# Two transformer blocks on one core: a new order of steps, the residual on VectorE, and GpSimd's low parts in halves

## The chip, the cores and the metric

The kernel runs on one NeuronCore of a Trainium2 chip, in one launch. Its engines are TensorE (PE), VectorE (DVE), ScalarE (ACT), GpSimd (POOL) and SyncE (SP), which issues transfers. The metric is the time on the device of one launch in microseconds (us), lower is better.

## The reference, cut to what matters

256 tokens of width 1024 go through two kinds of block, each with two layers. A layer is a feed-forward part, a mixer and a second feed-forward part.

```
f = (silu(h @ w_gate) * (h @ w_up)) @ w_down          # width 2816
block 1:  h = h + 0.5 * rms_norm(f);  u = rms_norm(h)
          y_a: short convolution   y_b: convolution over 31 tokens
          y_c: difference of two softmaxes, 4 heads, rms_norm   y_d: attention with decay, 8 heads
          h = h + rms_norm((g0*y_a + g1*y_b + g2*y_c + g3*y_d) @ w_o)
block 2:  x = layernorm(alpha * x + 0.5 * f, g, b)
          y_a: attention in a window of 128, 16 heads
          q, k, v = silu(convolution over 4 tokens);  y_b: gated delta rule, 8 heads, chunks of 64
          x = layernorm(alpha * x + (g_a*y_a + g_b*y_b) @ w_out, g, b)
```

## The kernel before, in words

**Numbers.** Every large product in float32 is made as three products of a reduced type: high by high, low by high and high by low. Weights come from memory in units (1 MB, or 768 KB for the gates of block 1) into a ring of four slots. ScalarE rounds a unit to `weights_high` (L1537). `weights_low`, the difference, is made by VectorE (L1862), or by GpSimd (`split_low`, L908) for most projection and gate units of block 2's mixer. A unit is split in four quarters.

**Order.** `plan_first` and `plan_second` write out a list of steps for each block, and every engine walks the list of its block in that order and does its own part of each step. Each engine has one queue: what stands behind a waiting instruction waits too. `interleave` weaves a chain of small steps (attention, the solve of the delta rule) with the rounds of dense products: behind each item of the chain stand some rounds. A product in pieces is a `part`. What VectorE does with a finished product (`later`) is put behind the next items of the chain, one each.

**Feed-forward part** (`plan_ffn`). 22 gate/up products `gu` (TensorE L1044), 11 `down` products of two gates each. Between them ScalarE makes the silu and VectorE the product and its high and low parts (L1903, L1869, L1871). L1101 is a `down` product, and L1112 (`last_rows`) the last one, in which each result is completed in turn. L1112 also completes the mixer's output product `wo`.

**First mixer.** Chain: heads of branch c (score, turn, value), then its squares on ScalarE, reciprocal roots on GpSimd and scaling on VectorE (`out_norm`, L2105), then branch d. Dense: projections `dq`, `dk`, `dv`, the projections of branch a (`value_a`, `gate_a`) and gates (L1346); a gate unit of block 1 ends with the product of a branch's output (L1349).

**Block 2.** `affine` on GpSimd (L935, L937) makes the residual of each stage, g*x + b. Second mixer: `ps` and `cumg` make the decays (TensorE L1388, VectorE L2198 to L2203), then comes attention (score L1242, softmax, turn L1257), then pairs of heads of the delta rule. Preparation of a head: `dtr` (transposes, L1402), `dte` (reciprocal root on GpSimd, scaling on VectorE, L2255 to L2266), `ddc`, `dtf`, `dkk`. `dtr` of a head needs three convolutions: `pconv` on TensorE (L1132), `taps` (L2230, L2232) and `silu` (L2245) on VectorE. The solve of a pair: `dl0`, then levels `dla`, `dlb` (L1457; masks by L2318), `du1` to `du4`, `dot`. The next pair's preparation is put into the solve.

## Time and profile before

| | |
|---|---|
| median of 3 runs | 3339.35 us (3338.19 to 3339.7) |
| profiled execution, its own time | 3333.8 us |
| span of its records | 3332.1 us |
| mean granted clock of TensorE | 0.959 |
| stages: feed-forward; mixer 1; feed-forward (layer 0 of block 1) | 0 to 219; 219 to 578; 578 to 784 us |
| the same, layer 1 | 784 to 988; 988 to 1344; 1344 to 1549 |
| feed-forward; mixer 2; feed-forward (layer 0 of block 2) | 1549 to 1772; 1772 to 2242; 2242 to 2446 |
| the same, layer 1 | 2446 to 2649; 2649 to 3120; 3120 to 3332 |

The profile is that of one execution, and its own time is 5.5 us under the median. Times in the rows count from the start of the span. In a row of the timeline the first number is the start, the second the duration, and the bracket says how long the engine was idle before and what released it. The matmul records overlap, and some of them can be missing.

### The profile page before, as it was taken

To read this page: it belongs to the slowest core of one execution; us is meant where nothing else is said; L and a number is where in the kernel's file an instruction comes from. 1 tells how busy PE (TensorE), PEld (TensorE's weight loads), DVE (VectorE), ACT (ScalarE), POOL (GpSimd) and SP (SyncE) were. 2 spreads that over 40 slices of the span, in tenths; PEclk is the share of its full clock that TensorE was granted. 3 is DMA by queue.
4 is the path that set the end of the run, shared out by engine and by line. 5 is a ranking of instruction groups with operands and counts; after the bars stand their busy time and mean duration, and the time that the engine had idled before them with its cause. 6 is when DMAs were issued, how large, how long until landed. Compare 5 with 4: busy or idle time off the path is not lost.

```text
span 3332.1 us, 59102 instructions
## 1 busy us (share of the span) xinstructions
PE 3070.4 (92%) x22178; PEld 2901.9 (87%) x22178; DVE 1944.3 (58%) x3310; ACT 1341.5 (40%) x2224; POOL 532.0 (16%) x471
## 2 busy tenths in 40 slices
PE   8989999998989999998898978989989998889998
PEld 7989898998989999897797877989979888789897
DVE  4556776555556876554554576466565536654755
ACT  4344454434344454432333534434333345433332
POOL 0000000000000000001103444431010044444300
PEclk9999999999999999998898999999999989999999
DMA  5544444554544445456552321255545422123453
GB/s 207 182 159 153 132 144 168 176 188 148 189 158 154 142 142 171 165 186 150 198 202 102 102 77 54 87 177 181 190 162 200 160 100 89 64 66 138 170 188 127
DMA packets 72442, 495.49 MB, mean 149 GB/s; under 512 B 8064, under 2 KB 8240, under 8 KB 20176
## 3 DMA queue, kind: packets, MB, share of 16 engines
q1 hardware_dynamic: 67824, 471.95, 41.5%
q0 software_dynamic: 4048, 18.59, 2.1%
q8 instruction: 184, 3.01, 0.4%
q14 instruction: 114, 0.93, 0.1%
q10 hardware_dynamic: 272, 0.99, 0.1%
HBM read 487.31 MB, written 4.19 MB: 148 GB/s over the span
## 4 chain that ended last, share of the span: by engine, by line
issue 74%; PE 12%; DVE 6%; POOL 4%; POOLq 2%; DVEq 2%; ACT 1%; DMA 0%; ACTq 0%; SPq 0%
PE psum L1132 4%; POOL weights_low L908 2%; DVE work L2232 1%; PE psum L1346 1%; PE psum L1352 1%; POOL small L867 1%; POOLq L936 1%; PE psum L1242 1%; POOL residual L937 1%; POOLq L866 1%; DVE small L2257 0%; PE psum L1188 0%; DVE work L2318 0%; PE psum L1457 0%; DVEq L2235 0%
## 5 line engine op out<-in xcount | busy, mean ns | idle before, releaser
L1537 ACT ACTIVATE weights_high<-weight_ring 128x2048 fp32r<-128x2048 f32 (+3 forms) x788 | 906.8, 1171 | 1105.0 <-DMA weight_ring<-stream 1097.6
L1862 DVE TENSOR_TENSOR weights_low<-weight_ring,weights_high 128x2048 fp32r<-128x2048 f32 (+6 forms) x532 | 906.6, 1710 | 757.3 <-ACT weights_high L1537 753.8
L1044 PE MATMUL psum<-normed_t_high,weights_high 128*128 128x256 f32 x2816 | 802.5, 285 | 11.6 <-DVE normed_t_low L1871 10.5
L1044 PE MATMUL psum<-normed_t_low,weights_high 128*128 128x256 f32 x2816 | 800.2, 284 | 0.0
L1044 PE MATMUL psum<-normed_t_high,weights_low 128*128 128x256 f32 x2816 | 799.6, 284 | 0.0
L1044 PEld LDWEIGHTS psum<-normed_t_high,weights_high 128*128 128x128 f32 x2816 | 542.9, 193 | 17.4 <-DVE normed_t_low L1871 11.8
L1044 PEld LDWEIGHTS psum<-normed_t_low,weights_high 128*128 128x128 f32 x2816 | 543.9, 193 | 3.6
L1044 PEld LDWEIGHTS psum<-normed_t_high,weights_low 128*128 128x128 f32 x2816 | 543.6, 193 | 0.0
L1101 PE MATMUL psum<-weights_high,work_parts 128*128 128x512 f32 x1472 | 464.5, 397 | 19.5 <-DVE work_parts L1871 19.5
L1132 PE MATMUL psum<-normed_t_high,weights_high 128*128 128x256 f32 x1248 | 394.8, 316 | 3.2 <-DVE normed_t_low L1871 2.1
L908 POOL TENSOR_TENSOR weights_low<-weight_ring,weights_high 128x512 fp32r<-128x512 f32 (+1 forms) x216 | 346.2, 1618 | 274.6 <-ACT weights_high L1537 274.6
L1132 PE MATMUL psum<-normed_t_low,weights_high 128*128 128x256 f32 x1248 | 361.3, 290 | 0.0
L1132 PE MATMUL psum<-normed_t_high,weights_low 128*128 128x256 f32 x1248 | 360.7, 289 | 0.0
L865 POOL TENSOR_TENSOR small<-small 128x1 f32<-128x1 f32 (+3 forms) x74 | 18.9, 256 | 2107.5 <-ACT work L1585 992.6
L1101 PEld LDWEIGHTS psum<-weights_high,work_parts 128*128 128x128 f32 x1472 | 271.0, 189 | 77.8 <-DVE work_parts L1871 19.9
L1101 PE MATMUL psum<-weights_low,work_parts 128*128 128x512 f32 x736 | 290.9, 395 | 0.0
L1132 PEld LDWEIGHTS psum<-normed_t_high,weights_high 128*128 128x128 f32 x1248 | 248.0, 199 | 17.4 <-issue 11.3
L1346 PE MATMUL psum<-normed_t_high,weights_high 128*128 128x256 f32 x768 | 236.5, 308 | 14.8 <-DVE weights_low L1862 9.4
L1132 PEld LDWEIGHTS psum<-normed_t_low,weights_high 128*128 128x128 f32 x1248 | 248.5, 199 | 1.1
L1132 PEld LDWEIGHTS psum<-normed_t_high,weights_low 128*128 128x128 f32 x1248 | 247.0, 198 | 0.0
L1346 PE MATMUL psum<-normed_t_low,weights_high 128*128 128x256 f32 x768 | 222.5, 290 | 0.0
L1346 PE MATMUL psum<-normed_t_high,weights_low 128*128 128x256 f32 x768 | 222.2, 289 | 0.0
(268 smaller groups left out, 4477.5 us busy)
## 6 DMA issues: line engine op xcount, KB each, us to landing
weight_ring<-stream SPq DMA_DIRECT2D x400, 1024.0 KB, 4.9
weight_ring<-stream SPq DMA_DIRECT2D x64, 768.0 KB, 4.2
feature_rows<-feat POOLq DMA_DIRECT2D x6, 1024.0 KB, 5.1
work<-toeplitz_rows POOLq DMA_DIRECT2D x8, 512.0 KB, 6.6
feature_rows<-feat POOLq DMA_DIRECT2D x6, 512.0 KB, 3.8
toeplitz_rows<-work POOLq DMA_DIRECT2D x1, 3072.0 KB, 36.4
params<-prms POOLq DMA_DIRECT2D x5, 251.5 KB, 3.3
residual<-x SPq DMA_DIRECT2D x2, 512.0 KB, 4.3
```

Source lines behind the costliest of these rows:

```text
L866: pool.drain()
L867: pool.tensor_tensor(dst, dst, HALFNEG[:, 0:dst.shape[1]], ALU.pow).then_inc(signal, 1)
L908: pool.tensor_tensor(some(LOW, i, q, n), some(RING, i, q, n), some(HIGH, i, q, n).bitcast(F32), ALU.subtract).then_inc(low_by_pool, n)
L936: pool.drain()
L937: pool.tensor_tensor(H[:, t, :], H[:, t, :], PG[:, 1, :], ALU.add).then_inc(residual_ready, 1)
L1044: ins = pe.matmul(PS[:, bank, at:at + S], w[a][:, first + k, c * P:(c + 1) * P], src[b][:, k, :], start=(k, m) == (0, 0), stop=(k, m) == ( ...
L1101: ins = pe.matmul(PS[:, b, :], src[c][:, r, t * P:(t + 1) * P], w[a][:, r, n * HALF:(n + 1) * HALF], start=start and m == 0, stop=False, s ...
L1132: ins = pe.matmul(PS[:, job.bank, c * S:(c + 1) * S], w[i][:, k, c * P:(c + 1) * P], XT[j][:, k, :], start=(k, m) == (0, 0), stop=(k, m) = ...
L1242: ins = pe.matmul(dst, q[:, t * P:(t + 1) * P], k[:, 0:keys], start=True, stop=not extra, skip_group_check=True)
L1346: ins = pe.matmul(PS[:, job.bank, 0:S], w[p][:, r, 0:P], XT[q][:, r, :], start=(r, m) == (0, 0), stop=(r, m) == (KB - 1, 2), skip_group_ch ...
L1537: return act.activation(dst, src, ACT.Copy, scale=scale)
L1862: dve.tensor_tensor(some(LOW, i, q, n), some(RING, i, q, n), some(HIGH, i, q, n).bitcast(F32), ALU.subtract).then_inc(low_by_vector, n)
```

## The change

The steps of both blocks are put in another order: the last two gates stand ahead of the last two `down` products, and likewise for `gate` and `wo`; in the first mixer `dv` moves behind the products of branch a, and squares and root of branch c become a step `out_square` with items of branch d between it and `out_norm`. In block 2 the residual is made by VectorE in four pieces per stage, spread over the stage. In the second mixer `cumg` moves from ahead of the first score into the attention, each tap is a step of its own, two of which may stand behind an item, the two heads of a pair are prepared side by side, the scaling of `du4` becomes a step `dsc`, and gates and projections are dealt out anew. GpSimd makes each quarter of a low part in two instructions.

```diff
                 signals=[("gate_silu_ready", 1), ("hidden_ready", 1)])
-        if j >= 2 and j % 2 == 0:
+        if 2 <= j < FB - 2 and j % 2 == 0:
             down(j // 2 - 1)
         for kind, signals, args in after:
             if j in args["j"]:
                 pl.step(kind, signals=signals, s=s, j=j, p=args["j"].index(j))
+    down(FP - 2)
     down(FP - 1)
 
...
         f()
-        if later:
-            later.pop(0)()
+        for _ in range(2 if len(later) > 4 else 1):
+            if later:
+                later.pop(0)()
         passed += w
         upto = total * passed // weight
...
-    chain.append((3, lambda: pl.step("out_norm", ("on", "c"), br="c",
-                                     signals=[("out_squares_summed", 1), ("out_rsqrt_ready", 1)])))
-    chain.append((2, out_turn("c")))
+    squares = (1, lambda: pl.step("out_square", "out_square",
+                                  signals=[("out_squares_summed", 1), ("out_rsqrt_ready", 1)]))
+    out_norm = (1, lambda: pl.step("out_norm", ("on", "c"), br="c"))
...
-    chain += chain_d[:8]
+    chain += [squares] + chain_d[:2] + [out_norm] + chain_d[2:3] + [(2, out_turn("c"))] + chain_d[3:8]
...
-    dense = [(16, lambda what=what, p=p: project(what, p)) for what in ("dq", "dk", "dv") for p in range(2)]
+    chain += [(2, lambda: pl.step("out_norm", ("on", "d"), br="d")), (2, out_turn("d"))]
+    dense = [(16, lambda what=what, p=p: project(what, p)) for what in ("dq", "dk") for p in range(2)]
     dense += [(16, lambda p=p: gate_a(p)) for p in range(4)] + [(16, lambda p=p: value_a(p)) for p in range(2)]
+    dense += [(16, lambda p=p: project("dv", p)) for p in range(2)]
...
-    pl.steps += [gate(24)[0], gate(25)[0]]
+    pl.steps += [gate(j)[0] for j in range(24, 28)]
     acc = pl.step("acc", ("acc", 1), banks=acc_hi, s=1)
-    for k in range(2, KB + 1, 2):
-        if k < KB:
-            pl.steps += [gate(24 + k)[0], gate(24 + k + 1)[0]]
-        pl.step("wo", ("wo", k // 2 - 1), k=k // 2 - 1, unit=("wo", k // 2 - 1), src=("gy", 24 + k - 2))
+
+    def wo(k):
+        pl.step("wo", ("wo", k), k=k, unit=("wo", k), src=("gy", 24 + 2 * k))
+
+    pl.steps += [gate(j)[0] for j in range(28, 30)]
+    wo(0)
+    pl.steps += [gate(j)[0] for j in range(30, 32)]
+    for k in range(1, 4):
+        wo(k)
...
-        plan_ffn(pl, s, [("bias", [("bias_loaded", 16)], {"j": (3, 7, 11, 15)})] if s == 0 else [])
+        beside = [("affine", [("residual_ready", 1)], {"j": (4, 6, 8, 10)}),
+                  ("feature", [("feature_rows_loaded", 16)], {"j": (12,)})]
+        if s == 0:
+            beside.append(("bias", [("bias_loaded", 16)], {"j": (3, 7, 11, 15)}))
+        plan_ffn(pl, s, beside)
...
+        rest = []
+        for c in range(2):
+            for n in range(3):
+                rest.append(lambda c=c, n=n: pl.step("tap", hp=hp, w=w, p=c, a=n))
+            rest.append(lambda c=c: pl.step("taps", ("taps", hp, w, c), hp=hp, w=w, p=c, a=3,
+                                            signals=[("conv_ready", 1), ("conv_tanh_ready", 1)]))
+        rest.append(lambda: pl.step("silu", ("silu", hp, w), hp=hp, w=w, signals=[("conv_silu_ready", 1)]))
+        return host, rest
...
     pl.step("pk", "pk", banks=["lo"], unit=("w", 4))
+    affine(1, 0)
     pl.step("ps", "ps", banks=["lo"],
             signals=[("small_proj_ready", 1), ("small_logs_ready", 1), ("log_decay_ready", 1)])
     for p in range(2):
         pl.steps.append(query(p)[0])
+        affine(1, 1 + p)
     pl.step("pv", "pv", banks=["lo"], unit=("w", 5))
-    pl.step("cumg", "cumg", banks=["s"],
-            signals=[("decay_diff_ready", 1), ("decay_exps_ready", 1), ("decay_scalars_ready", 1)])
+    affine(1, 3)
...
+    def prepare(hs, banks):
+
+        steps = []
+
+        def add(h, kind, banks, signals=()):
+            steps.append(lambda: pl.step(kind, (kind, h), banks=banks, h=h, signals=signals))
+
+        for h, b in zip(hs, banks):
+            add(h, "dtr", b, [("qk_squares_summed", 1), ("qk_rsqrt_ready", 1)])
+            add(h, "dte", [], [("head_scalars_ready", 1)])
+        for h, b in zip(hs, banks):
+            add(h, "ddc", [3], [("decay_ready", 1), ("strict_decay_ready", 1)])
+            add(h, "dtf", b)
+        for h in hs:
+            add(h, "dkk", [3], [("level_masked", 1)])
+        return steps
...
+        for h in hs:
+            steps.append(lambda h=h: pl.step("dsc", ("dsc", h), h=h))
         both("dot", [("delta_out_ready", 1)])
         return steps
 
     steps, last = attention()
-    first = [prepare(0, (6, 7, 3)), prepare(1, (4, 5, 3))]
-    chain = steps + [(4, first[0][0])] + last + [(4, f) for f in first[0][1:2] + first[1][:1] + first[0][2:4]
-                                               + first[1][1:2] + first[0][4:] + first[1][2:]]
+    steps.insert(9, (2, lambda: pl.step("cumg", "cumg", banks=["s"],
+                                        signals=[("decay_diff_ready", 1), ("decay_exps_ready", 1),
+                                                 ("decay_scalars_ready", 1)])))
+    first = [(4, f) for f in prepare((0, 1), ((6, 7), (4, 5)))]
+    chain = steps + first[:1] + last + first[1:]
     dense = [(16, lambda p=p: query(p)) for p in (2, 3)] + [(16, lambda w=w: conv(0, w)) for w in range(3)]
     dense += [(16, lambda p=p: gated(p)) for p in range(2)] + [(16, lambda w=w: conv(1, w)) for w in range(3)]
+    dense += [(16, lambda: gate(0, 0, "lo3"))]
     interleave(pl, chain, dense)
 
     pairs = NH_B // 2
-    extra = [[(16, lambda: gate(0, 0, "lo3"))] + [(16, lambda w=w: conv(2, w)) for w in range(3)],
-             [(16, lambda: gate(0, 1, "lo3"))] + [(16, lambda w=w: conv(3, w)) for w in range(3)],
-             [(16, lambda p=p: gated(p)) for p in (2, 3)] + [(16, lambda k=k: gate(0, k, "lo3")) for k in (2, 3)],
-             [(16, lambda k=k: gate(0, k, "lo3")) for k in range(4, 8)]]
+    extra = [[(16, lambda w=w: conv(2, w)) for w in range(3)] + [(16, lambda: gate(0, 1, "lo3"))],
+             [(16, lambda w=w: conv(3, w)) for w in range(3)] + [(16, lambda: gated(2))],
+             [(16, lambda: gated(3))] + [(16, lambda k=k: gate(0, k, "lo3")) for k in range(2, 5)],
+             [(16, lambda k=k: gate(0, k, "lo3")) for k in range(5, 8)]]
     for hp in range(pairs):
         chain = [(2, f) for f in solve((2 * hp, 2 * hp + 1))]
         if hp + 1 < pairs:
-            todo = [f for h in (2 * hp + 2, 2 * hp + 3) for f in prepare(h, (6, 7, 3))]
-            for n, f in enumerate(todo):
-                chain.insert(2 + 3 * n, (2, f))
+            todo = [(2, f) for f in prepare((2 * hp + 2, 2 * hp + 3), ((6, 7), (6, 7)))]
+            ends = chain[-4:]
+            chain = chain[:-4]
+            for n, item in enumerate(todo[:8]):
+                chain.insert(2 + 4 * n, item)
+            chain += todo[8:] + ends
         interleave(pl, chain, extra[hp])
...
                     pool.wait_ge(high_ready, reach("high_ready", QUARTERS * i + q + n))
-                    pool.tensor_tensor(some(LOW, i, q, n), some(RING, i, q, n), some(HIGH, i, q, n).bitcast(F32),
-                                       ALU.subtract).then_inc(low_by_pool, n)
+                    w = width(i) // QUARTERS // 2
+                    for part in range(2 * q, 2 * (q + n)):
+                        at = (slice(None), i % SLOTS, slice(part * w, (part + 1) * w))
+                        ins = pool.tensor_tensor(LOW[at], RING[at], HIGH[at].bitcast(F32), ALU.subtract)
+                        if part % 2:
+                            ins.then_inc(low_by_pool, 1)
 
             def norm(st):
...
+            def affine(st):
+
+                if st.p == 0:
+                    dve.wait_ge(feature_rows_loaded, reach("feature_rows_loaded", 16 * st.s))
+                t, cols = st.p // 2, slice(st.p % 2 * HALF, (st.p % 2 + 1) * HALF)
+                dve.tensor_tensor(H[:, t, cols], XN[:, t, cols], PG[:, 0, cols], ALU.mult)
+                dve.drain()
+                dve.tensor_tensor(H[:, t, cols], H[:, t, cols], PG[:, 1, cols], ALU.add).then_inc(residual_ready, 1)
+                dve.drain()
...
 
-            def du4(st):
-                job, i = st.jobs[0], st.h % 2
-                dve.wait_ge(out_rsqrt_ready, reach("out_rsqrt_ready", st.at["out_rsqrt_ready"]))
+            def dsc(st):
+                done, i = named(("du4", st.h)), st.h % 2
+                job = done.jobs[0]
+                dve.wait_ge(out_rsqrt_ready, reach("out_rsqrt_ready", done.at["out_rsqrt_ready"]))
                 for t in range(T):
```

**The end of a feed-forward part, on TensorE.** L1044 before is L1065 after (a gate), L1101 is L1122 (a `down` product), L1112 is L1133 (the last one). Before, from the end of `down` 9 through gate 21 to the last rows:

```order
L1101 MATMUL psum<-weights_low,work_parts 128x512
L1029 REGISTER_ALU
L1074 REGISTER_ALU
L1044 MATMUL psum<-normed_t_high,weights_high 128x256
L1044 MATMUL psum<-normed_t_low,weights_high 128x256
L1044 MATMUL psum<-normed_t_high,weights_low 128x256
...
L1084 REGISTER_ALU
L1112 MATMUL psum<-weights_high,work_parts 128x512 x2
L1112 MATMUL psum<-weights_low,work_parts 128x512
```

After, from the start of gate 21 on:

```order
L1050 REGISTER_ALU
L1095 REGISTER_ALU
L1065 MATMUL psum<-normed_t_high,weights_high 128x256
L1065 MATMUL psum<-normed_t_low,weights_high 128x256
L1065 MATMUL psum<-normed_t_high,weights_low 128x256
...
L1109 REGISTER_ALU
L1122 MATMUL psum<-weights_high,work_parts 128x512 x2
L1122 MATMUL psum<-weights_low,work_parts 128x512
...
L1105 REGISTER_ALU
L1133 MATMUL psum<-weights_high,work_parts 128x512 x2
```

What moved: the `down` product now stands between the last gate and the last rows, where before the last rows followed the gate directly.

**VectorE ahead of the solve of heads 2 and 3, behind which `dtr` of head 4 stands.** Before: the end of `dot` of head 1 (L1871), the taps (L2230, L2232) of the last convolution, silu (L2245), and `dl0` (L2304, L2306):

```order
L1871 TENSOR_TENSOR work_parts<-work,work_parts 128x256
L2230 TENSOR_SCALAR work<-psum,params 128x256
L2232 SCALAR_TENSOR_TENSOR work<-psum,params,work 128x255
L2232 SCALAR_TENSOR_TENSOR work<-psum,params,work 128x254
L2232 SCALAR_TENSOR_TENSOR work<-psum,params,work 128x253
L2242 REGISTER_ALU
L2245 SCALAR_TENSOR_TENSOR work<-work 128x512
L2302 REGISTER_ALU
L2304 TENSOR_TENSOR work<-constants,psum 128x128 x2
L2306 TENSOR_TENSOR work<-constants,work 128x128 x2
```

After: L2260 is a tap, L2274 the silu, L2320 and L2325 are `dkk`, L2356 is `dsc`, L2363 `dot`, L2333 and L2335 are `dl0`:

```order
L2260 SCALAR_TENSOR_TENSOR work<-psum,params,work 128x253
L2271 REGISTER_ALU
L2274 SCALAR_TENSOR_TENSOR work<-work 128x512
L2320 TENSOR_TENSOR work<-psum,work 128x512
L2325 TENSOR_TENSOR work<-work,constants 128x128 x2
L2356 TENSOR_SCALAR work<-psum,small 128x128 x4
L2363 SCALAR_TENSOR_TENSOR work<-psum,small,work 128x256
L1888 CAST work_parts<-work 128x256
L1890 TENSOR_TENSOR work_parts<-work,work_parts 128x256
L2333 TENSOR_TENSOR work<-constants,psum 128x128 x2
L2335 TENSOR_TENSOR work<-constants,work 128x128 x2
```

What moved: taps and silu stand ahead of `dkk` and `dot`, and nothing stands between `dot` and `dl0` but one operation of a gate.

**TensorE at the start of the attention in block 2.** Before: `cumg` (L1387 to L1390), then the first score (L1242) and the woven projection (L1132):

```order
L1387 MATMUL psum<-small,constants 128x16
L1388 MATMUL psum<-small,constants 128x16
L1390 MATMUL psum<-constants,small 8x128 x2
L1233 REGISTER_ALU
L1242 MATMUL psum<-work 128x128
L1242 MATMUL psum<-work 128x256
L1132 MATMUL psum<-normed_t_high,weights_high 128x256
L1132 MATMUL psum<-normed_t_low,weights_high 128x256
L1132 MATMUL psum<-normed_t_high,weights_low 128x256
```

After: `cumg` (L1408 to L1411) within the projection (L1153), and the values of a head behind it (L1307):

```order
L1153 MATMUL psum<-normed_t_high,weights_low 128x256
L1408 MATMUL psum<-small,constants 128x16
L1409 MATMUL psum<-small,constants 128x16
L1411 MATMUL psum<-constants,small 8x128 x2
L1153 MATMUL psum<-normed_t_high,weights_high 128x256
L1153 MATMUL psum<-normed_t_low,weights_high 128x256
L1153 MATMUL psum<-normed_t_high,weights_low 128x256
L1307 MATMUL psum<-work 128x64
```

What moved: `cumg` no longer precedes the first score but follows the third head's turn.

## Rows read from the trace of the kernel before

**Rows 1.** The page, section 1: busy time of each engine.

```profile
PE 3070.4 (92%) x22178; PEld 2901.9 (87%) x22178; DVE 1944.3 (58%) x3310; ACT 1341.5 (40%) x2224; POOL 532.0 (16%) x471
```

**Rows 2.** Waits of TensorE by line: total us, times, longest us.

```profile
PE psum L1402 <- DVE work L2245: 31.6, 6, 5.5
...
PE psum L1112 <- DVE work_parts L1871: 18.5, 10, 2.0
PE psum L1457 <- DVE work L2318: 11.2, 10, 1.6
...
PE psum L1349 <- DVE work_parts L1871: 6.9, 2, 3.4
```

**Rows 3.** Windows of TensorE's granted clock: us, busy time by engine, PEclk.

```profile
core 0: us, PE busy (x) PEld busy (x) DVE busy (x) ACT busy (x) POOL busy (x), PEclk, DMA share, GB/s
376.60:383.40 6.80, 6.09 (x28) 6.10 (x29) 6.59 (x13) 2.84 (x6) 0.00 (x0) 0.50 0.27 69
384.00:394.00 10.00, 10.00 (x87) 10.00 (x86) 5.55 (x12) 3.56 (x8) 0.00 (x0) 1.00 0.34 101
769.10:772.50 3.40, 3.40 (x10) 2.65 (x9) 0.00 (x0) 0.00 (x0) 0.00 (x0) 0.50 0.59 178
1997.90:2004.70 6.80, 4.34 (x21) 4.34 (x22) 3.37 (x12) 3.03 (x12) 0.81 (x2) 0.50 0.00 0
```

**Rows 4.** Groups of GpSimd by line and shape: busy us, mean ns, idle before.

```profile
L908 POOL TENSOR_TENSOR weights_low<-weight_ring,weights_high 128x512 fp32r<-128x512 f32 x192 | 244.5, 1291 | 203.9 <-ACT weights_high L1537 203.8
L908 POOL TENSOR_TENSOR weights_low<-weight_ring,weights_high 128x2048 fp32r<-128x2048 f32 x20 | 92.1, 4604 | 57.9 <-ACT weights_high L1537 57.9
L935 POOL TENSOR_TENSOR residual<-work,feature_rows 128x1024 f32<-128x1024 f32 x12 | 41.0, 3416 | 53.4 <-DVE normed_t_low L1871 53.4
```

**Rows 5.** The same groups, of VectorE.

```profile
L1871 DVE TENSOR_TENSOR work_parts<-work,work_parts 128x256 fp32r<-128x256 f32 x224 | 115.7, 517 | 17.8 <-issue 1.4
L1862 DVE TENSOR_TENSOR weights_low<-weight_ring,weights_high 128x512 fp32r<-128x512 f32 x60 | 40.3, 686 | 2.3 <-ACT weights_high L1537 2.3
```

**Rows 6.** Timeline at 1816: start us, duration us, then idle time before.

```profile
1816.23 4.54 POOL L908 TENSOR_TENSOR weights_low<-weight_ring,weights_high 128x2048 fp32r<-128x2048 f32 x1 [1.02 <-ACT weights_high L1537]
...
1816.42 4.38 DVE L2203 TENSOR_TENSOR small<-small 128x16 f32<-128x16 f32 x1
...
1823.81 0.90 PE L1257 MATMUL psum<-constants,work 128*128 128x128 f32 x3 [4.58 <-ACT work L1650]
```

**Rows 7.** Timeline of the first feed-forward part of block 2, at 1588.

```profile
1588.75 3.81 DVE L1862 TENSOR_TENSOR weights_low<-weight_ring,weights_high 128x2048 fp32r<-128x2048 f32 x1 [21.56 <-ACT weights_high L1537]
...
1594.91 2.34 POOL L937 TENSOR_TENSOR residual<-residual,feature_rows 128x1024 f32<-128x1024 f32 x1
1595.00 2.54 DVE L1871 TENSOR_TENSOR work_parts<-work,work_parts 128x256 fp32r<-128x256 f32 x1
1597.46 2.28 DVE L1862 TENSOR_TENSOR weights_low<-weight_ring,weights_high 128x2048 fp32r<-128x2048 f32 x1
...
1597.59 1.22 PE L1101 MATMUL psum<-weights_high,work_parts 128*128 128x512 f32 x2 [19.49 <-DVE work_parts L1871]
```

**Rows 8.** Timeline of the first mixer at 402.

```profile
402.27 1.29 DVE L2105 TENSOR_TENSOR work<-psum,small 128x512 f32<-128x512 f32 x2 [5.07 <-POOL small L867]
...
404.56 0.57 PE L1346 MATMUL psum<-normed_t_high,weights_high 128*128 128x256 f32 x1 [4.02 <-DVE weights_low L1862]
```

**Rows 9.** Timeline of the second mixer, 1994 to 2011.

```profile
1994.93 0.48 DVE L2230 TENSOR_SCALAR work<-psum,params 128x256 f32<-128x256 f32 x1
...
2005.13 1.25 DVE L2255 TENSOR_SCALAR small<-small 128x2 f32<-128x2 f32 x1 [3.22 <-POOL small L867]
...
2009.06 0.60 DVE L2266 TENSOR_SCALAR feature_rows<-psum,small 128x128 f32<-128x128 f32 x2
...
2010.68 0.71 PE L1457 MATMUL psum<-work 128*128 128x128 f32 x4 [0.77 <-DVE work L2318]
```

**Rows 10.** Window of the preparation of the first two heads.

```profile
1904.00:1935.00 31.00, 23.07 (x169) 22.07 (x167) 27.48 (x67) 13.73 (x38) 16.45 (x16) 0.91 0.33 115
```

123 lines of the change are left out of this document (46 added, 77 removed).

## The prediction

> **What bounds the kernel now.** I read the page's busy times first [rows 1]: TensorE is busy 3070.4 of 3332.1 us (92%), VectorE 58%, ScalarE 40%, GpSimd 16%. No other engine comes near its limit over the whole span, and the change removes no matmul. So all that can be won is what TensorE loses: 262 us in which it stands still (3332.1 - 3070.4), and the time in which it runs at half its clock. The second view is therefore the list of TensorE's waits [rows 2], and the third the windows that show its clock [rows 3]. In 376.60:383.40, right behind a wait of 3.4 us, the granted clock is 0.50 (1.2 GHz), and 28 matmul records fit into 6.8 us. At 1.00 (2.4 GHz) 87 fit into 10.0 us, that is 59 in 6.8. A wait of this kind costs twice, then: itself, and about 3.0 us of the window behind it (half of the 6.1 us in which TensorE works there). The waits of some 4 to 5 us at 404, 1823 and 2000 have such windows too; behind the 1.9 us at 768.6 comes one of 3.4 us, worth 1.7. The work ahead of each wait is what I price.
>
> **Last gates ahead of last rows (ten places: eight feed-forward parts and, by the new order of `gate` and `wo`, the outputs of block 1's two mixers).** `down` 10 starts with the rows of gate 21, whose silu, product and split were begun only when gate 21's last matmul ended. L1112 waits for that split, 18.5 us in ten waits [rows 2], 1.85 each. Now `down` 9 lies between (24 matmuls of 512 columns, each two of the 0.115 us that 10.0/87 gives for 256 columns: 5.5 us) and covers the 1.85 fully. The half-clock windows at 769.1 and (alike, after the wait at 564.4) in the mixer go with them, 2 x 1.7. Other such waits are shorter or run into the window of the normalization that follows, and bring nothing more. **Sum -21** (18.5 + 3.4, less one for what stays).
>
> **First mixer (twice).** Two things stand here. The gate at 377.3 waits 3.43 for branch a's product on VectorE (L1349, 6.9 in two) [rows 2]; with `dv` dealt behind value_a and gate_a, two projections of 16 rounds of three matmuls (48 x 0.115 = 5.5 us each) lie ahead of it. At 404.6 L1346 waits 4.02 for `weights_low`. That stands behind L2105 in VectorE's queue, and L2105 waits 5.07 for the reciprocal root of branch c, which GpSimd makes from ScalarE's squares [rows 8]. The change makes squares and root a step of their own, and puts two items of branch d with their share of matmuls between them and L2105. That is over 5 us of TensorE's work. Both waits have a 6.8 us window at 0.50. Sum: 6.9 + 2 x 4.02 + 4 x 3.0 = 26.9, less 1 for a rest: **-26**.
>
> **Residual on VectorE.** GpSimd loses 12 instructions L935 of 1024 columns, 41.0 us [rows 4], and as many of L937. VectorE gets 24 pieces of two 128x512 operations at 0.69 us [rows 5], with the drain 1.5 us each: 36 us. They stand beside gates 4, 6, 8 and 10 of a feed-forward part and between the first projections of the mixer. VectorE is at 58% there and the next `weights_low` is made over 5 us ahead of its use, so I cost them at 0; without that cover they would be +36. At one place the removal pays: in the first feed-forward of block 2 TensorE waits 19.49 us [rows 7], mostly because the weights come late behind the 3 MB transfer of the bias rows, but the end of it is VectorE: L1862 takes 3.81 there and L1871 2.54, beside GpSimd's L935 and L937 (one of 2.34 is shown), while the same forms take 2.28 a moment later [rows 7] and 0.52 in the mean [rows 5]. (3.81 - 2.28) + (2.54 - 0.52) = 3.6: **-4**. The new wait of VectorE for the constants ends inside the same stall.
>
> **Start of the attention in block 2 (twice).** GpSimd's L908 of 2048 columns runs from 1816.23 for 4.54 us, and VectorE's L2203, 16 columns wide, from 1816.42 for 4.38 us: both end together at 1820.8 [rows 6]. The softmax of the first head stands behind it in VectorE's queue, and TensorE waits 4.58 for it at 1823.8, and a window at 0.50 as long as that of 376.60 lies behind; TensorE works through all of it, so it loses 3.4. After the change `cumg`, to which L2203 belongs, is no longer ahead of the first score, and GpSimd's pieces are 256 columns. Two prices are known [rows 4]: 1291 ns for 512 columns, 4604 for 2048. Their line is 2.16 us per 1000 columns plus 0.19 us, so 0.74 us for 256, between the bounds 0.65 (half of 1291) and 1.29 (no cheaper). The longest block becomes 0.7 us. 2 x (4.58 - 0.6 + 3.4) = 14.8: **-15**.
>
> The Trainium skill (SBUF — State Buffer, Who interferes with whom) says that GpSimd and VectorE share one port pair, that whoever issues first keeps it for the whole instruction, and that only instructions of VectorE with two SBUF inputs or in a two-port mode are held. The trace agrees in L2203 (4.38 us beside 4.54). By that rule the halving shortens each block to a sixth here, but lets a `weights_low` of VectorE (2.3 us) hold GpSimd eight times per unit and not once, which the sum leaves out.
>
> **Second mixer, solve and preparation (twice).** L1402, the transposition of two new heads, waits 31.6 in six waits for the silu L2245 [rows 2]: the eight tap instructions of a projection (0.48 us each [rows 9], some 4 us) and the silu are in VectorE's queue right ahead of it, as they are begun only when the projection ends. For pairs 2 and 3 the taps now lie in the solve before, a few matmuls apart, and the silu ahead of `dkk`. Four of the six waits go, 21, and four windows at 0.50 with 4.34 us of matmuls [rows 3], 4 x 2.2. The first of each layer stays, since its taps still stand directly ahead. Of L1457's 11.2 I give 4. In the preparation of the first pair (1904 to 1935) VectorE is the bound, busy 27.48 of 31 us [rows 10]; three of its instructions per head are held by GpSimd for about 1 us each, so 3.7 per layer, 7.4. Gross: 21 + 9 + 4 + 7 = 41. Against it stands `dte`: it waits 3.22 for GpSimd's root and then takes until 2009.7, about 4.5 us [rows 9]. It now lies between the two heads' `dlb` steps, whose masks (L2318) the next matmuls need. I take 60% of the gross: **-25**.
>
> **New small waits.** Gates of block 2 at the mixer's end come back to back at 5.5 to 5.7 us; GpSimd took 4.6 for a unit and now takes 8 x 0.74 = 5.9. Eight units a layer at 0.2 are 3 us, and as much for waits of the new weave: **+6**. [...]
>
> **Sum.** -21 - 26 - 4 - 15 - 25 + 6 = -85. The profiled execution took 3333.8, so 3249. The median is 3339.35, 5.5 higher, as it was for before: **3254**, 2.6% less.
>
> **The rivals.** (a) *The gaps of the second mixer only move.* For it: VectorE is the bound in the preparation, and `dte` is put into the solve. Against it: the taps need not be made at one go any more. The -25 becomes 0: 3279. 0.17. (b) *All of it comes*, since VectorE is held less everywhere: -41 in the second mixer and no +6: 3232. 0.15. (c) *Branch c's root comes late as before*, because VectorE's queue order and not the distance decides: 2 x (4.02 + 3.0) = 14 return, 3268. 0.10. (d) *Slower:* the 12 `dte` steps woven into solves each stop TensorE. TensorE waits their whole length at L1457, as VectorE does nothing else meanwhile, 4.5 us, and each wait brings a 6.8 us window at 0.50, 3.0 more. 12 x 7.5 = 90 on top of (a): 3369. It turns slower than before when a `dte` costs over (3339 - 3279) / 12 = 5.0 us. Against it: the same `dte` at 2005 to 2009.7 left only a wait of 0.77 at TensorE [rows 9]. 0.04. (e) *The halves cost 1.29 us each.* A unit then takes 10.3 against 5.7, and for 16 units at the ends of the mixers that is 74: 3325. The two durations in [rows 4] speak against it. 0.04. My forecast, within 12 us of 3254, has the remaining 0.50.
>
> **Range and chances.** 3228 to 3290: it takes in (a), (b) and (c) and leaves out (d) and (e), with some room. Differences under 0.2% can't be told from none. Faster by more 0.94, within 0.2% 0.02, slower 0.04.
>
> **What the profile after would show.** L1112's waits gone (18.5 to under 1), no wait for `weights_low` or `work_parts` over 2 us in 219:578, L1257 from 9.2 to under 2, L1402 from 31.6 to about 10; GpSimd with some 560 instructions of 128x256 at 0.74 us and no residual; the mean clock from 0.959 to about 0.97. Wrong would be: L1457 waiting over 20 us behind L2255, a `weights_low` by GpSimd among TensorE's releasers, or VectorE's residual pieces ahead of a late `weights_low`.

## The result, and the profile after

The changed kernel takes 3260.35 us in the median of 4 runs (3257.02 to 3263.16), beside 3338.77 for the kernel before on the same chip (3333.43 to 3339.7): 0.9768 of its time, 95% interval 0.9751 to 0.9785. Its profiled execution took 3261.25, with a span of 3259.6 and a mean granted clock of 0.966. The forecast was 3254 with a range of 3228 to 3290. By the medians the gain is 78.4 us. The two profiled executions, on which all sums below rest, differ by 72.5, because that of the kernel before (3333.8) was 5.0 us under this median and that of the changed kernel 0.9 over its own.

Line numbers have moved: L1044 is now L1065, L1101 L1122, L1112 L1133, L1132 L1153, L1402 L1423, L1257 L1278, L1457 L1478, L1862 L1881, L1871 L1890, L2131 L2150, L908 L942. First the page's busy times (section 1), which answer to [rows 1]:

```profile
PE 3045.4 (93%) x22178; PEld 2883.8 (88%) x22178; DVE 1881.4 (58%) x3364; ACT 1340.2 (41%) x2214; POOL 524.2 (16%) x791
```

TensorE's busy time fell by 25.0 us although it does the same 22178 matmuls. Most of that is the clock: TensorE worked 188.6 us at a granted clock of 0.50 before and 147.0 after, and half of the difference is 20.8 us. The other 47.5 us of the 72.5 by which the span got shorter were idle time. These are the waits by line (total, times, longest), beside [rows 2]. First four more lines of the kernel before:

```profile
PE psum L1063 <- DVE work L2161: 19.6, 8, 3.7
...
PE psum L1508 <- DVE work L2326: 8.8, 16, 1.1
...
PE psum L1428 <- DVE work L2291: 5.3, 2, 2.7
...
PE psum L1063 <- issue: 4.2, 1, 4.2
```

and the changed kernel:

```profile
PE psum L1084 <- DVE work L2188: 27.3, 9, 4.7
...
PE psum L1529 <- DVE work L2356: 12.4, 8, 1.7
PE psum L1478 <- DVE work L2347: 11.7, 10, 1.7
PE psum L1423 <- DVE work L2274: 11.5, 2, 5.7
PE psum L1449 <- DVE work L2304: 11.0, 2, 5.5
...
PE psum L1170 <- DVE weights_low L1881: 9.4, 2, 4.7
...
PE psum L1278 <- ACT work L1671: 1.8, 2, 1.0
```

L1133's wait is gone from the list (18.5 before), L1423 fell from 31.6 to 11.5, and L1278 from 9.2 (two of 4.6) to 1.8. One large wait is new: 9.4 at L1170, in the first mixer. The wait at L1449 (L1428 before), in the preparation of the hybrid mixer, which is the second mixer, grew from 5.3 to 11.0, and that at L1529 (L1508 before) from 8.8 to 12.4. L1084's wait for the layer normalization seems to grow from 19.6 to 27.3, but the list counts nine waits where it had eight. The ninth, 4.7 us at the end of a feed-forward part, stood before under "issue" with 4.2. Counted alike, 23.8 became 27.3. GpSimd's and VectorE's groups by shape, beside [rows 4]:

```profile
L942 POOL TENSOR_TENSOR weights_low<-weight_ring,weights_high 128x256 fp32r<-128x256 f32 x560 | 410.6, 765 | 223.3 <-ACT weights_high L1558 223.3
```

```profile
L2150 DVE TENSOR_TENSOR work<-work 128x256 f32<-128x256 f32 x64 | 31.7, 495 | 5.9
```

A half takes 765 ns in the mean and 734 in the median (0.74 was forecast). The mean holds halves of up to 1858 ns; eight in a row that were not drawn out took 5.5 us. L2150 adds the gated output of one branch to the sum of the others, and both inputs are in on-chip memory. Before (L2131) it took 962 ns in the mean, with a median of 425: a few of the 64 were drawn out, up to 4336 ns.

The stages by the start of each one's first transposition (TensorE L1061 and L1063 before), in us, added up by kind. The last column divides the prediction's terms over them (7 x 1.85 + 1.7; 26 + 2 x 1.85 + 1.7 - 1; 4 + 1.85; 15 + 25 - 6):

| | before | after | change | forecast |
|---|---|---|---|---|
| seven feed-forward parts | 1453.9 | 1441.1 | -12.8 | -14.6 |
| two first mixers | 714.8 | 702.4 | -12.4 | -30.4 |
| first feed-forward part of block 2 | 223.1 | 216.2 | -6.9 | -5.9 |
| two hybrid mixers | 940.3 | 899.8 | -40.5 | -34 |

The first mixers gave 18 us less than forecast and the hybrid mixers 6.5 more. The rows of the first mixer, at 362 to 368, VectorE and TensorE (start, duration, idle before):

```profile
362.35 0.69 DVE L1881 TENSOR_TENSOR weights_low<-weight_ring,weights_high 128x512 fp32r<-128x512 f32 x1
363.13 0.62 DVE L2030 TENSOR_SCALAR work<-work,params 128x256 f32<-128x256 f32 x2
363.82 1.83 DVE L2032 SCALAR_TENSOR_TENSOR work<-work,params 128x255 f32<-128x255 f32 x4
365.73 0.69 DVE L2037 TENSOR_TENSOR work<-work,psum 128x512 f32<-128x512 f32 x1
366.51 0.43 DVE L1888 CAST work_parts<-work 128x512 fp32r<-128x512 f32 x1
367.01 0.69 DVE L1890 TENSOR_TENSOR work_parts<-work,work_parts 128x512 fp32r<-128x512 f32 x1
367.62 0.69 DVE L1881 TENSOR_TENSOR weights_low<-weight_ring,weights_high 128x512 fp32r<-128x512 f32 x1
```

```profile
368.36 0.58 PE L1170 MATMUL psum<-weights_high,normed_t_high 128*128 128x256 f32 x1 [4.71 <-DVE weights_low L1881]
```

VectorE has hardly any idle time here. The low part L1881 at 362.35 is followed by the convolution and product of branch a (L2030 to L1890, five microseconds), and only then by the next quarter's low part, for which the projection dv (L1170) waits 4.71. Around its end lies a stretch of half clock (length, busy time of TensorE, its weight loads, VectorE, ScalarE and GpSimd, granted clock, share and rate of the transfers):

```profile
366.00:372.80 6.80, 4.44 (x21) 4.44 (x22) 6.28 (x16) 1.33 (x5) 0.00 (x0) 0.50 0.35 116
```

In the hybrid mixer the preparation of the first two heads looks like this, VectorE first:

```profile
1876.69 0.48 DVE L2259 TENSOR_SCALAR work<-psum,params 128x256 f32<-128x256 f32 x1 [2.41 <-PE psum L1423]
1877.26 0.48 DVE L2260 SCALAR_TENSOR_TENSOR work<-psum,params,work 128x255 f32<-128x255 f32 x1
1877.66 0.60 DVE L2284 TENSOR_SCALAR small<-small 128x2 f32<-128x2 f32 x1
...
1885.60 0.68 DVE L2284 TENSOR_SCALAR small<-small 128x2 f32<-128x2 f32 x1 [3.06 <-POOL small L898]
```

```profile
1890.15 0.80 PE L1449 MATMUL psum<-work,constants 128*128 128x256 f32 x1 [5.49 <-DVE work L2304]
```

The tap L2259 at 1876.69 waits 2.41 for the transposition of head 1 (L1423). Head 0's scaling (from L2284 on) stands behind this tap. So head 1's squares and root come late, its L2284 waits 3.06 for GpSimd, and TensorE waits 5.49.

The end of a feed-forward part of block 2:

```profile
1737.56 2.29 DVE L1881 TENSOR_TENSOR weights_low<-weight_ring,weights_high 128x2048 fp32r<-128x2048 f32 x1 [2.80 <-ACT weights_high L1558]
1739.77 0.68 DVE L2177 SCALAR_TENSOR_TENSOR work<-psum,residual 128x512 f32<-128x512 f32 x1
```

```profile
1745.47 0.90 PE L1084 MATMUL psum<-constants,work 128*128 128x128 f32 x3 [4.62 <-DVE work L2188]
```

The next unit's low part waits 2.80 for its high part, whose weights had just come, and the normalization (L2177) stands behind it in VectorE's queue.

### The profile page after: what moved, and what is told of

The parts are those of the page before. It is cut to its first block, busy times and chain, and to the rows that moved or that the text cites. A ratio compares the mean times of both kernels' runs of the same rounds, so it can differ in the third digit from the quotient of the medians.

```text
span 3259.6 us, 59469 instructions
## 1 busy us (share of the span) xinstructions
PE 3045.4 (93%) x22178; PEld 2883.8 (88%) x22178; DVE 1881.4 (58%) x3364; ACT 1340.2 (41%) x2214; POOL 524.2 (16%) x791
## 4 chain that ended last, share of the span: by engine, by line
issue 71%; PE 16%; POOL 5%; DVE 4%; DVEq 1%; ACT 1%; POOLq 1%; DMA 1%; ACTq 0%; SPq 0%
PE psum L1153 5%; POOL weights_low L942 4%; PE psum L1065 4%; PE psum L1122 1%; PE psum L1263 1%; POOL small L898 1%; DMA weight_ring<-stream 1%; PE psum L1490 1%; DVE work L2260 1%; POOLq L897 1%; PE psum L1367 1%; PE psum L1209 1%; PE psum L1488 0%; PE psum L1478 0%; ACT weights_high L1558 0%
## 5 line engine op out<-in xcount | busy, mean ns | idle before, releaser
L1558 ACT ACTIVATE weights_high<-weight_ring 128x2048 fp32r<-128x2048 f32 (+5 forms) x778 | 906.0, 1184 | 1121.1 <-DMA weight_ring<-stream 1113.9
L1881 DVE TENSOR_TENSOR weights_low<-weight_ring,weights_high 128x2048 fp32r<-128x2048 f32 (+4 forms) x538 | 888.1, 1658 | 789.7 <-ACT weights_high L1558 786.8
L1065 PE MATMUL psum<-normed_t_high,weights_high 128*128 128x256 f32 x2816 | 801.4, 285 | 11.3 <-DVE normed_t_low L1890 9.9
L1065 PE MATMUL psum<-normed_t_low,weights_high 128*128 128x256 f32 x2816 | 798.9, 284 | 0.0
L1065 PE MATMUL psum<-normed_t_high,weights_low 128*128 128x256 f32 x2816 | 798.6, 284 | 0.0
L1065 PEld LDWEIGHTS psum<-normed_t_high,weights_high 128*128 128x128 f32 x2816 | 541.7, 192 | 17.7 <-DVE normed_t_low L1890 12.3
L1065 PEld LDWEIGHTS psum<-normed_t_low,weights_high 128*128 128x128 f32 x2816 | 542.4, 193 | 3.2
L1065 PEld LDWEIGHTS psum<-normed_t_high,weights_low 128*128 128x128 f32 x2816 | 542.1, 193 | 0.0
L1122 PE MATMUL psum<-weights_high,work_parts 128*128 128x512 f32 x1472 | 464.1, 397 | 13.5 <-DVE work_parts L1890 13.5
L942 POOL TENSOR_TENSOR weights_low<-weight_ring,weights_high 128x256 fp32r<-128x256 f32 x560 | 410.6, 765 | 223.3 <-ACT weights_high L1558 223.3
L1153 PE MATMUL psum<-normed_t_high,weights_high 128*128 128x256 f32 x1248 | 392.1, 314 | 2.8 <-DVE normed_t_low L1890 2.1
L1153 PE MATMUL psum<-normed_t_low,weights_high 128*128 128x256 f32 x1248 | 359.2, 288 | 0.0
L1153 PE MATMUL psum<-normed_t_high,weights_low 128*128 128x256 f32 x1248 | 358.6, 287 | 0.0
L1122 PEld LDWEIGHTS psum<-weights_high,work_parts 128*128 128x128 f32 x1472 | 271.0, 189 | 72.2 <-DVE work_parts L1890 14.0
L896 POOL TENSOR_TENSOR small<-small 128x1 f32<-128x1 f32 (+3 forms) x74 | 19.4, 263 | 1893.9 <-ACT work L1606 977.3
L1122 PE MATMUL psum<-weights_low,work_parts 128*128 128x512 f32 x736 | 290.7, 395 | 0.0
L1153 PEld LDWEIGHTS psum<-normed_t_high,weights_high 128*128 128x128 f32 x1248 | 245.8, 197 | 17.2 <-issue 11.9
L1153 PEld LDWEIGHTS psum<-normed_t_low,weights_high 128*128 128x128 f32 x1248 | 246.0, 197 | 1.0
L1153 PEld LDWEIGHTS psum<-normed_t_high,weights_low 128*128 128x128 f32 x1248 | 244.7, 196 | 0.0
## 6 DMA issues: line engine op xcount, KB each, us to landing
toeplitz_rows<-work POOLq DMA_DIRECT2D x1, 3072.0 KB, 36.6
```

The lines of the kernel that those rows point to most:

```text
L942: ins = pool.tensor_tensor(LOW[at], RING[at], HIGH[at].bitcast(F32), ALU.subtract)
L1065: ins = pe.matmul(PS[:, bank, at:at + S], w[a][:, first + k, c * P:(c + 1) * P], src[b][:, k, :], start=(k, m) == (0, 0), stop=(k, m) == ( ...
L1122: ins = pe.matmul(PS[:, b, :], src[c][:, r, t * P:(t + 1) * P], w[a][:, r, n * HALF:(n + 1) * HALF], start=start and m == 0, stop=False, s ...
L1153: ins = pe.matmul(PS[:, job.bank, c * S:(c + 1) * S], w[i][:, k, c * P:(c + 1) * P], XT[j][:, k, :], start=(k, m) == (0, 0), stop=(k, m) = ...
L1558: return act.activation(dst, src, ACT.Copy, scale=scale)
L1881: dve.tensor_tensor(some(LOW, i, q, n), some(RING, i, q, n), some(HIGH, i, q, n).bitcast(F32), ALU.subtract).then_inc(low_by_vector, n)
```

## The experiments

A ratio is that to the kernel before on the same chip, with its 95% interval. Where two of these kernels are compared, the lengths of their stages in the profiles are set beside each other. A profile is one execution, and it can lie some us off the median.

**e1: the order of the last gates alone.** The kernel before, with:

```diff
-        if j >= 2 and j % 2 == 0:
+        if 2 <= j < FB - 2 and j % 2 == 0:
             down(j // 2 - 1)
...
+    down(FP - 2)
     down(FP - 1)
```

and the new order of `gate` and `wo` in block 1. Expected:

> The kernel before, with only the new order of the last gates ahead of the last down products, and of gate and wo in block 1. Theory (the order takes away the wait ahead of the last rows, but in block 2 part of it comes back, since the next unit's low part, late behind its transfer, stands ahead of the normalization in VectorE's queue): the ten waits of L1112, 18.5 us, are gone; the four feed-forward parts of block 1 get shorter by 1.9 each, those of block 2 by under 1 on average while TensorE's wait for L2161 grows from 19.6 to about 25; the whole is faster by 12 to 16 us, near 3325. Rival (all of the wait is won, as my prediction had it): faster by 20 or more, near 3317, and the wait for L2161 stays at 19.6.

Measured: 3311.55, 0.9922 (0.9905 to 0.9939), 26 us by the medians. In the profile the span is 20.0 shorter: 18.3 in the eight feed-forward parts and 2.1 in each first mixer, less 2.5 in the hybrid mixers. Of these the one in layer 0 got 3.0 longer, though its steps are the same. The rival, which was the prediction's own step, is nearer in the time: even in block 2 the parts get 0.5 to 3.1 shorter, 1.9 in the mean. But the wait for the normalization did grow, from 19.6 to 22.4 in eight waits, as the theory said, if by less.

**e2: GpSimd in whole quarters.** The changed kernel, with:

```diff
-                    w = width(i) // QUARTERS // 2
-                    for part in range(2 * q, 2 * (q + n)):
-                        at = (slice(None), i % SLOTS, slice(part * w, (part + 1) * w))
-                        ins = pool.tensor_tensor(LOW[at], RING[at], HIGH[at].bitcast(F32), ALU.subtract)
-                        if part % 2:
-                            ins.then_inc(low_by_pool, 1)
+                    pool.tensor_tensor(some(LOW, i, q, n), some(RING, i, q, n), some(HIGH, i, q, n).bitcast(F32),
+                                       ALU.subtract).then_inc(low_by_pool, n)
```

> The changed kernel, with GpSimd's low parts in whole quarters again, one instruction for several quarters where they come together. Theory (long instructions of GpSimd hold VectorE): L2150 (the attention's 128x256 product) goes back from 495 ns in the mean to about 960, and both hybrid mixers get longer by 3 to 8 us each, so 3260 becomes 3266 to 3276. Rival (the halves only add fixed cost on GpSimd, and the gain came from the order): the same or up to 6 us faster than the changed kernel.

Measured: 3285.73, 0.9851 (0.9832 to 0.9870). The halves are worth some 25 us, more than the theory's 6 to 16. The mixers are 461.5 and 466.0 against 450.9 and 448.9. Of these 27.7 us, 12.7 lie in the attention, ahead of the first transposition for the delta rule, 5.0 in the preparation of the first pair, and 9.9 in the solves and behind them. L2146, the addition above, is back at 1019 ns in the mean. At the start of the attention, though `cumg` has moved, VectorE is still held (timeline, GpSimd, VectorE, TensorE):

```profile
1787.16 4.51 POOL L939 TENSOR_TENSOR weights_low<-weight_ring,weights_high 128x2048 fp32r<-128x2048 f32 x1 [0.96 <-ACT weights_high L1554]
```

```profile
1787.46 4.24 DVE L2065 TENSOR_SCALAR small<-small 128x2 f32<-128x2 f32 x1
```

```profile
1792.85 0.90 PE L1274 MATMUL psum<-constants,work 128*128 128x128 f32 x3 [3.65 <-ACT work L1667]
```

An instruction on 2 columns takes 4.24 us, and ends with GpSimd's. In the solves the waits are only slightly longer, but the clock is not the same. Two waits of e2 that answer to L1529 and L1478 above:

```profile
PE psum L1525 <- DVE work L2352: 14.4, 8, 2.1
...
PE psum L1474 <- DVE work L2343: 12.9, 10, 2.1
```

and windows of 70 us over the same kind of steps of layer 1 (columns as in [rows 3]), of e2, with one of the three stretches of half clock in it:

```profile
2838.00:2908.00 70.00, 62.01 (x473) 60.42 (x474) 45.42 (x138) 28.90 (x92) 27.77 (x31) 0.93 0.22 76
2838.90:2842.30 3.40, 3.40 (x18) 3.40 (x17) 2.88 (x8) 0.75 (x2) 0.00 (x0) 0.50 0.00 0
```

and of the changed kernel:

```profile
2820.00:2890.00 70.00, 61.31 (x506) 59.47 (x506) 48.97 (x155) 31.14 (x99) 34.40 (x53) 1.00 0.23 76
```

The changed kernel's waits there are 1.7 at most and its clock is 1.00. Those of e2 reach 2.1 and its clock is 0.93: four stretches of 3.4 us at 0.50 lie in the solves of its layer 1, none of that length in those of the other. In layer 0 of e2, with the same waits, there is only one. So the longer waits go with more half clock here, but do not bring it each time.

**e8: the halves alone, on the kernel before.** The edit of e2 turned round:

```diff
-                    pool.tensor_tensor(some(LOW, i, q, n), some(RING, i, q, n), some(HIGH, i, q, n).bitcast(F32),
-                                       ALU.subtract).then_inc(low_by_pool, n)
+                    w = width(i) // QUARTERS // 2
+                    for part in range(2 * q, 2 * (q + n)):
+                        at = (slice(None), i % SLOTS, slice(part * w, (part + 1) * w))
+                        ins = pool.tensor_tensor(LOW[at], RING[at], HIGH[at].bitcast(F32), ALU.subtract)
+                        if part % 2:
+                            ins.then_inc(low_by_pool, 1)
```

> The kernel before, with only GpSimd's low parts in halves. Theory (long instructions of GpSimd hold VectorE, and the waits so drawn out are those behind which TensorE's clock falls): the wait of 4.58 at L1257 falls under 1.5 without any change of order, L2131 falls from 962 to about 490 ns, and the hybrid mixers get 8 to 12 us shorter each: 3315 to 3323. Rival (the halves pay only together with the new order of taps, since the first run without them lost 25 us there): under 8 us in all, 3331 and more.

Measured: 3315.30, 0.9924 (0.9908 to 0.9941). That is 25 us by the medians and 15.4 in the profile, which is of the slowest of its four executions. L1257's two waits fell from 9.2 to 5.1, L2131 from 962 to 496 ns, and the mixers from 470.1 and 470.3 to 461.9 and 462.1, 8.1 each. Only 1.2 and 1.1 of that lie in the attention. The theory holds in the time, and in the mixers at the lower end of its 8 to 12. At L1257 it does not: 2.6 is left of 4.6 where it said under 1.5, and a stretch of 10.2 us at 0.50 still begins there in both layers; `cumg` is still ahead of the first score. In this order the gain is idle time (55.9 became 46.8 us in the mixer of layer 0), not clock.

**e6: `cumg` ahead of the first score again,** in the changed kernel:

```diff
     affine(1, 3)
+    pl.step("cumg", "cumg", banks=["s"],
+            signals=[("decay_diff_ready", 1), ("decay_exps_ready", 1), ("decay_scalars_ready", 1)])
     def attention():
...
-    steps.insert(9, (2, lambda: pl.step("cumg", "cumg", banks=["s"],
-                                        signals=[("decay_diff_ready", 1), ("decay_exps_ready", 1),
-                                                 ("decay_scalars_ready", 1)])))
```

> The changed kernel, with cumg ahead of the first score of the hybrid mixer again, and GpSimd still in halves. Theory (the halves alone end the wait at the start of the attention, since with whole quarters and cumg moved it was still 3.65): L1257's successor L1278 waits under 1.5, no window at 0.50 follows, and the time is within 3 us of 3260. Rival (cumg's place decides): a wait of 3 to 4.6 with its window comes back in both layers, 10 to 15 us slower.

Measured: 3266.03, 0.9783 (0.9766 to 0.9799), 5 us more by the medians and 2.9 in the span. L1277 waits 1.9 and 2.7, the second with 3.4 us of half clock beginning beside it. That is more than the theory's 1.5 and less than the rival's 3 to 4.6. So both parts of the change act on this wait: with whole quarters 3.65 was left, with `cumg` at its old place 1.9 to 2.7, with both 1.0.

**e5: dv ahead of gate_a and value_a again,** in the changed kernel:

```diff
-    dense = [(16, lambda what=what, p=p: project(what, p)) for what in ("dq", "dk") for p in range(2)]
+    dense = [(16, lambda what=what, p=p: project(what, p)) for what in ("dq", "dk", "dv") for p in range(2)]
...
-    dense += [(16, lambda p=p: project("dv", p)) for p in range(2)]
```

> The changed kernel, with the projections dv of the first mixer ahead of gate_a and value_a again. Theory (moving dv only moved the wait: VectorE's work for branch a's product now stands ahead of a low part of dv, where before it stood ahead of the gate's rows): L1170's two waits of 4.71 go, L1370's two waits of 3.4 come back, the stages of the first mixer stay within 2 us of 352.5 and 350.0, and the time within 4 us of 3260. Rival (the move was worth its share of my prediction, 6 us a layer): about 3272.

Measured: 3261.34, 0.9765 (0.9749 to 0.9781), the same as the changed kernel. The stages are 351.6 and 353.5 against 352.4 and 350.0. In place of L1170's wait there are two, first of the gate's own low part and then of branch a's product:

```profile
369.46 0.38 PE L1366 MATMUL psum<-normed_t_high,weights_high 128*128 128x256 f32 x1 [2.33 <-DVE weights_low L1880]
...
377.14 0.50 PE L1369 MATMUL psum<-work_parts,weights_high 128*128 128x256 f32 x2 [3.90 <-DVE work_parts L1889]
```

The theory holds, with the difference that two waits come back and not one of 3.4.

**e3: the taps of branch a as steps of their own,** in the changed kernel:

```diff
     def gate_a(p):
+        rest = [lambda n=n: pl.step("tap_a", p=p, a=n) for n in range(3)]
-        return pl.make("pa", ("pa", p), banks=["lo"], signals=[("branch_gate_ready", 1)], p=p, unit=("aa", p)), []
+        return pl.make("pa", ("pa", p), banks=["lo"], signals=[("branch_gate_ready", 1)], p=p, unit=("aa", p)), rest
...
+            def tap_a(st):
+                c, n = st.p, st.a
+                dve.drain()
+                w = prm("aw", 1, 3)[:, 2 - n, c:c + 1]
+                if n == 0:
+                    dve.tensor_scalar(ACCA[:, c, :], ZA[:, c, :], w, None, ALU.mult)
+                else:
+                    dve.scalar_tensor_tensor(out=ACCA[:, c, n:S], in0=ZA[:, c, 0:S - n], scalar=w,
+                                             in1=ACCA[:, c, n:S], op0=ALU.mult, op1=ALU.add)
```

> The changed kernel, with the six tap operations of branch a's convolution taken out of the step of its product and made steps of their own behind each gate_a, so that 5.3 us of VectorE's work no longer stand in one piece ahead of a low part of dv. Theory (that block is what L1170 waits for): the wait of 4.71 at 368 and its half-clock window go in both layers, stages of the first mixer 352.5 and 350.0 get shorter by 6 to 8 us each, 3260 becomes about 3246. Rival (the low part is late for its transfer, or VectorE is simply full there): the wait stays, or comes back elsewhere in the mixer, and the time stays within 3 us of 3260.

Measured: 3256.18, 0.9757 (0.9740 to 0.9773). The wait fell from 4.71 to 2.12 in both layers, and no half clock lies behind it. Taken from the start of this matmul to the end of the mixer, each layer is 1.8 shorter, and the wait itself 2.6. But the stages are 348.4 and 350.1. At the start of the mixer the stretch of half clock is 10.2 us in one of the two layers and 6.8 in the other, in both kernels, but they have changed places. That adds 1.7 to the gain of the first and takes 1.7 from that of the second; what took the rest there is not shown. A part of both: VectorE's block was the cause of the wait, and product and split still stand ahead of the low part.

**e4: dtr of head 1 ahead of dte of head 0,** in the changed kernel:

```diff
-    chain = steps + first[:1] + last + first[1:]
+    chain = steps + first[:1] + last + [first[2], first[1]] + first[3:]
```

> The changed kernel, with the transposition of head 1 (dtr) ahead of the scaling of head 0 (dte) in the preparation of the first pair. Theory (VectorE is not full there: its first tap of the next convolution waits for that transposition while head 0's scaling stands behind it, and head 1's scaling then waits for GpSimd's root): VectorE's waits of 2.41 and 3.06 at 1876 and 1885 go, the wait of 5.49 at L1449 falls under 2, and each hybrid mixer gets 3 to 6 us shorter, so about 3251. Rival (VectorE's work alone bounds this stretch, as my prediction had it): the waits move to the next step and the time stays within 2 us of 3260.

Measured: 3248.54, 0.9734 (0.9717 to 0.9751), 12 us under the changed kernel. The mixers are 443.0 and 442.4 against 450.9 and 448.9. L1449's wait has left the list, and VectorE's for GpSimd in L2284 too. From the first transposition of head 0 to that of head 2 it is 35.0 us, where it was 41.6 in the changed kernel and 36.1 before. The theory holds, and VectorE, busy 27.91 of 42 us in that stretch of the changed kernel, was not what bounds it:

```profile
1869.00:1911.00 42.00, 30.07 (x220) 29.05 (x221) 27.91 (x71) 18.42 (x52) 21.98 (x33) 0.89 0.29 101
```

and the same stretch of e4:

```profile
1869.00:1911.00 42.00, 34.17 (x253) 32.49 (x252) 31.34 (x80) 20.66 (x62) 26.42 (x39) 0.93 0.31 104
```

**e7: the next unit's low part behind the normalization** in block 2, in the changed kernel:

```diff
                 to_low = to_high
+                if st.kind == "post2" or any(x.kind == "post2" for x in self.steps[n + 1:n + 2]):
+                    to_low = low
```

> The changed kernel, with the low part of the next unit behind the layer normalization in VectorE's queue, at the ends of all parts of block 2. Theory (that low part is late behind its transfer and holds up the normalization, 3.4 us at 1739.77): TensorE's wait for L2188, 27.3 in all, falls to about 18, and each of the six ends gets 1 to 2 us shorter: 3250 to 3254. Rival (the low part is then late for the first product of the next stage): the wait moves to L1065 or L1153 and the time stays within 3 us of 3260.

Measured: 3252.32, 0.9738 (0.9722 to 0.9754), 8 us under the changed kernel, 9.3 in the span. TensorE's waits for the normalization are here

```profile
PE psum L1086 <- DVE work L2190: 14.3, 8, 2.4
...
PE psum L1086 <- issue: 4.1, 1, 4.1
```

Counted alike, 27.3 became 18.4. So the low parts ahead of the normalization stood on the path that sets the end.

**e9: e4, with three of the steps put off behind an item where more than eight stand in line.**

```diff
-        for _ in range(2 if len(later) > 4 else 1):
+        for _ in range(3 if len(later) > 8 else 2 if len(later) > 4 else 1):
```

> The run e4 (dtr of head 1 ahead of dte of head 0), and three of the steps put off (taps, silu) behind an item of the chain where more than eight stand in line. Theory (TensorE's wait of 5.7 at L1423, ahead of heads 2 and 3, is the rest of the taps, made in one piece since the few items of the preparation take too few of them): that wait falls under 3 and its half-clock window goes, 3 to 6 us per hybrid mixer, so about 3239 where e4 had 3248.5. Rival (VectorE is now full in the preparation): the taps hold up head 0's and 1's steps instead, the mixers stay at 443, and the time within 3 us of 3248.5.

Measured: 3252.25, 0.9745 (0.9726 to 0.9764), e4 had 3248.54. L1423's two waits fell from 11.5 only to 10.0, L1467 waits 3.8 where it hardly did, and the mixers are 447.1 and 445.2 where e4 had 443.0 and 442.4. The rival is nearer: part of the wait moved. By the intervals the two times can't be told apart.

**c1 and c2: all that paid, without and with the rule of e9.** c1 has e3, e4, e7, branch a's product put off behind the next item, and VectorE's wait for the constants moved into the first piece of the residual.

```diff
     def value_a(p):
+        def rest():
+            st = named_a[p]
+            pl.steps.append(Step("mul_a", None, src=st, p=p))
-        return pl.make("conva", ("conva", p), banks=["lo"], p=p, unit=("w", p), signals=[("branch_a_ready", 1)]), []
+        named_a[p] = pl.make("conva", ("conva", p), banks=["lo"], p=p, unit=("w", p), signals=[("branch_a_ready", 1)])
+        return named_a[p], [rest]
...
                 if st.p == 0:
+                    if st.s == 0:
+                        dve.wait_ge(zeros_set, 3)
...
-            dve.wait_ge(zeros_set, 3)
```

> The changed kernel with what paid so far: taps of branch a as steps of their own (e3), and its product, too, put off behind the next item; dtr of head 1 ahead of dte of head 0 (e4); the next unit's low part behind the layer normalization (e7); and VectorE's wait for the constants moved from the start of block 2 to the first piece of the residual. Theory (these waits are independent of each other): 3260 - 4 - 12 - 8 from the three runs, 2 to 4 more for the rest of the wait at L1170, and 2 for L1084's 8.8 back to 6.8: 3230 to 3235. Rival (they share one limit, such as the transfers of the weights): less than 18 in all, over 3242.

> The run c1 with the taps' rule of e9. Theory: what e9 wins over e4 is won here too, 6 to 12 us under c1, about 3224. Rival: nothing or a loss, as there.

Measured: c1 3238.68, 0.9702 (0.9688 to 0.9717); c2 3240.10, 0.9709 (0.9693 to 0.9724). c1 is the fastest kernel of the study, about 0.7% under the changed one. It gains 22 where the theory had 25 to 30. In block 2 the parts keep most of their gains (mixers 440.9 and 440.6), the feed-forward part with the constants is 202.8 for 205.2, and the first mixers gain nothing together (349.3 and 353.6). These are c1's waits:

```profile
PE psum L1093 <- DVE work L2199: 14.9, 8, 2.3
...
PE psum L1432 <- DVE work L2285: 11.5, 2, 5.7
...
PE psum L1376 <- DVE weights_low L1890: 5.1, 4, 2.1
PE psum L1376 <- DVE work L2154: 4.5, 2, 2.2
...
PE psum L1179 <- DVE weights_low L1890: 3.5, 2, 1.8
```

The wait at L1170 (here L1179) became two, 1.8 there and about 2.1 at L1376. And the time at half clock differs between layers that run the same steps. I took from the traces, for each stage, TensorE's idle time and the time in which it worked at 0.50; what is left of the length without the idle time and half of the latter moves less than the length:

| stage | length | idle | working at 0.50 | rest |
|---|---|---|---|---|
| first mixer, layer 1, after | 350.0 | 13.9 | 14.3 | 329.0 |
| the same, c1 | 353.6 | 14.2 | 19.4 | 329.7 |
| hybrid mixer, layer 1, before | 470.3 | 56.1 | 44.1 | 392.1 |
| the same, e8 | 462.1 | 47.1 | 48.4 | 390.9 |
| the same, e2 | 466.0 | 48.7 | 56.4 | 389.1 |
| the same, after | 448.9 | 43.1 | 31.3 | 390.2 |

For c1's first mixer that says where 3.6 us are: its idle time is that of the changed kernel, since a wait of 2.1 at L1376 came in for what L1170 lost, and it works 5 us more at half clock, worth 2.5. Why these stretches lie as they do stays open.

**e10: e1 and e8 together, on the kernel before,** with the two diffs shown there.

> The kernel before, with the new order of the last gates (e1) and GpSimd's low parts in halves (e8), and nothing else of the change. Theory (the two act at different places, so they add up): 0.9922 x 0.9924 = 0.985 of the time before, about 3287, with hybrid mixers of 462 us and the ten waits ahead of the last rows gone. What is left to the changed kernel, about 27 us, is then the work of the new order in the mixers and of the residual on VectorE. Rival (both shorten the same wait chains, or each moves the other's clock windows): 3295 or more.

Measured: 3295.08 beside 3341.09, 0.9855 (0.9822 to 0.9888). Spans: 20.0 for e1, 15.4 for e8, 36.6 for both. They add up, and so they do by the ratios (0.9922 x 0.9924 = 0.9847 beside 0.9855). The remaining 35.9 us to the changed kernel, 29 by the ratios, come from the mixers' new order and the residual together, which no run takes apart: 11.3 and 12.5 in the hybrid mixers, 4.3 and 3.2 in the first ones, 6.6 in the first feed-forward part of block 2, and 2.7 lost in the part ahead of it.

## Why the prediction was right or wrong

- **The bound.** That TensorE's idle time and its half clock are all there is to win held: both fell (47.5 and 20.8 us), and what is left of each stage without them moved by 2 us at most between before and after.
- **The number.** It came out 6 us from the forecast, and part of that is luck. The forecast for the profiled execution was 3249, and it took 3261. The 5.5 us that I added for the median did not come, as the changed kernel's profiled execution lay 0.9 over its median. And 18 us too few in the first mixers stand beside 6.5 too many in the hybrid ones.
- **Last gates ahead of last rows, -21.** Right: -20.0 in e1's profile (26 by its medians), and no wait is left at L1133. My later reading of the trace, that block 2 gives most of it back, was wrong: the wait for the normalization took back 2.8 (19.6 to 22.4). e7's 8 us are a second gain at the same place.
- **First mixer, -26.** The step that failed. It said that "both waits" go "less 1 for a rest". They did go, but L1349's came back as 4.71 at L1170, its half clock with it, and 1.3 at L1328. The prediction had named a wait over 2 us here as what the profile would not show. I had asked only what stands ahead of the gate on TensorE, not what VectorE's five microseconds for branch a stand ahead of in its own queue after the move. e5 shows that moving dv is worth nothing, e3 that cutting this block takes the wait from 4.71 to 2.12. From e1 to the changed kernel the mixers got 4.0 and 4.2 shorter: about the wait for branch c's root with its half clock (7), less what L1170 and L1328 have more than the wait at L1349 had. That is worked out from the waits; no run moves the root alone.
- **Residual on VectorE, 0 and -4.** Not contradicted, but no run has the residual alone. No wait points to the pieces, and the first part of block 2 went from 220.0 in e1 to 216.2. The same part was 222.8 in e10 and 220.8 in e8, so the 4 us are known to 2 or 3. What I had as hidden, the wait for the constants, is not: L1084's first wait in block 2 rose from 6.8 to 8.8, and c1, which moves it, has the 2 us back.
- **Start of the attention, -15.** The wait fell to 1.0 without half clock behind it, as forecast. From the start of the stage to the first transposition of a head, TensorE's idle time fell by 10.2 us in the two layers and its work at 0.50 by 12.4, worth 6.2: 16 us beside the forecast 15. e2, e6 and e8 show that neither part of the change does it alone. The rule of the Trainium skill on the shared port pair (SBUF — State Buffer, Who interferes with whom) agrees with e2's 4.24 us beside 4.51: the instruction of VectorE began 0.3 us behind GpSimd's and ended with it.
- **The halves outside the attention's start.** Not in the sum but for the 7 us of the preparation, and the largest thing missing in it. By the medians the halves are worth 25 us in either order (e2, e8). The mixers' profiles put 14 to 15 us of it behind the attention (14 of 16 in e8, 15 of 28 in e2). VectorE's instructions are drawn out less everywhere. With the old order that took idle time away (e8). With the new one it also turned waits of 2.1 in the solves into 1.7, and less half clock lies there (e2); that the one brings the other is argued, since the two layers of e2 differ with the same waits.
- **Second mixer, -25.** Right for the solves: L1402's 31.6 became 11.5 (about 10 was forecast), and the solves of the first two pairs take 58.6 and 56.8 us, from one pair's L1423 to the next, where it was 64.9 and 65.2. Wrong for the preparation: I took VectorE for the bound by its 27.48 of 31 us and counted a gain of 7.4, and it took 41.6 instead of 36.1, of which four more rounds of products explain 1.4. In the new order VectorE was waiting for a step behind which its own next work stood, as e4 shows. Whether it was the bound in the old order no run tests. That the two mixers came out 6.5 better than forecast is luck, then: the halves' gain, which the sum lacks, against this loss.
- **New waits, +6.** No run shows them apart. In the changed kernel GpSimd's slower units are not among TensorE's releasers. They are near it: in e4, e7 and e9, which are faster, TensorE waits 0.7, 2.3 and 2.8 us for them at the gates, 1.5 at most at once.
- **The rivals.** None of the five came, though the reason of (b), that VectorE is held less everywhere, is what e2 and e8 show. Of (d), that a wait at each woven `dte` costs 7.5, nothing shows: L1478 waits 11.7 in ten, where it was 11.2 in ten.

## What to carry to other kernels

Before counting a moved wait as won, read the queue of the engine that was late, from the late work to the next thing that another engine needs: the wait goes only if nothing needed stands behind that work. Do not price a stretch by the busy share that an engine had in the old order: in the new one look whether its idle time is a wait ahead of its own next needed work. And count the time at half clock beside the idle time. In e2 against the changed kernel it was more than half of the difference: 10.3 us of idle time and 18.9 of clock in the two hybrid mixers.

## What the runs showed of the hardware

- A VectorE instruction on 128x2 elements took 4.24 us beside a GpSimd instruction of 4.51 us and ended with it (e2); with GpSimd in pieces of 765 ns the same one took 0.66.
- A unit of GpSimd's work took 5.5 us in eight pieces that were not drawn out, and 7.5 where they were, against 4.6 in one. All of this work together kept GpSimd busy 410.6 us in pieces and 346 before, and the kernel was 25 us faster with the pieces.
- Most stretches of half clock were 3.4, 6.8, 10.2 or 13.7 us long. In the solves of layer 1 there was none of 3.4 with waits up to 1.7, and there were four with waits up to 2.1; in layer 0 one, with the same waits. A stage of the same steps had 3.4 us more or less of it from run to run, worth 1.7, and one hybrid mixer came out 3.0 longer with nothing changed in it (e1).
